# One register load for eight expert width marks on TensorE, in place of eight checked loads

## What is computed

```python
def moe_swiglu(x, router_w, w1, w3, w2):
    logits = (t @ router_w).astype(jnp.float32)
    top_v, top_i = lax.top_k(logits, TOP_K)
    gates = jax.nn.softmax(top_v, axis=-1)
    combine = jnp.sum(jax.nn.one_hot(top_i, N_EXPERTS) * gates[..., None], axis=1)
    for e in range(N_EXPERTS):
        out = out + combine[:, e:e + 1] * swiglu(t, w1[e], w3[e], w2[e])
```

## Time and profile before

| | us |
|---|---|
| median of 3 executions | 2331.02 |
| lowest, highest | 2330.19, 2338.54 |
| the profiled execution, own time | 2329.96 |
| the profiled execution, span from first to last instruction | 2328.0 |
| TensorE busy in the span | 2162.3 (93%) |
| VectorE, ScalarE, GpSimd busy | 1401.6, 1116.9, 1186.8 |

### The profile page before, as it was taken

The page is one execution under the profiler, slowest core; times in us unless marked ns, Lnnn a source line. Parts: engine busy times, 40 slices in busy tenths (PEclk is TensorE's granted clock), DMA queues, the critical chain, the costliest instruction groups (busy, mean ns, idle before and its releaser), DMA issues.

```text
span 2328.0 us, 26804 instructions
## 1 busy us (share of the span) xinstructions
PE 2162.3 (93%) x10612; PEld 1733.7 (74%) x10612; DVE 1401.6 (60%) x1775; ACT 1116.9 (48%) x1117; POOL 1186.8 (51%) x473
## 2 busy tenths in 40 slices
PE   8999899989997899999999999999899996878997
PEld 7578588875775677777778777888678773747997
DVE  4565643355656577777777775433477775455665
ACT  1232334312321576767676674434376772535544
POOL 0120154301200698989899895554398991203443
PEclk9999999989997899999999999999999997979999
DMA  8200464522004598989999896555399893215560
GB/s 303 72 1 18 166 222 156 199 96 73 1 27 166 214 362 326 366 310 360 331 344 360 318 361 223 181 181 183 144 356 358 319 357 122 105 36 187 194 215 21
DMA packets 208094, 484.93 MB, mean 208 GB/s; under 512 B 9168, under 2 KB 13008, under 8 KB 206928
## 3 DMA queue, kind: packets, MB, share of 16 engines
q1 hardware_dynamic: 207952, 483.02, 57.2%
HBM read 481.96 MB, written 1.05 MB: 207 GB/s over the span
## 4 chain that ended last, share of the span: by engine, by line
PE 85%; DVE 8%; ACT 2%; issue 2%; POOL 1%; DMA 1%; DVEq 0%; ACTq 0%; SPq 0%; POOLq 0%
PE bank L949 21%; PE bank L951 20%; PE bank L950 20%; PE bank L586 11%; PE bank L778 5%; PE bank L593 3%; DVE b_arena L1325 1%; PE bank L739 1%; DVE b_X L1325 1%; POOL b_arena L2632 1%; ACT e_hi L2168 1%; DVE b_arena L1331 1%; PE bank L856 1%; PE bank L695 1%; PE bank L1218 1%
## 5 line engine op out<-in xcount | busy, mean ns | idle before, releaser
L2725 POOL TENSOR_TENSOR e_lo<-b_ring,e_hi 128x512 fp32r<-128x512 f32 (+1 forms) x401 | 1122.2, 2819 | 634.6 <-ACT e_hi L2168 634.6
L1797 DVE TENSOR_TENSOR e_lo<-b_ring,e_hi 128x1536 fp32r<-128x1536 f32 (+2 forms) x407 | 781.6, 1921 | 472.2 <-ACT e_hi L2168 468.7
L2168 ACT ACTIVATE e_hi<-b_ring 128x2048 fp32r<-128x2048 f32 (+1 forms) x407 | 777.1, 1912 | 333.0 <-PE bank L951 327.0
L949 PE MATMUL bank<-e_hi,e_xh 128*128 128x512 f32 (+1 forms) x1200 | 475.9, 397 | 31.0 <-POOL e_lo L2725 9.4
L951 PE MATMUL bank<-e_hi,e_xl 128*128 128x512 f32 (+1 forms) x1200 | 466.3, 389 | 0.0
L950 PE MATMUL bank<-e_lo,e_xh 128*128 128x512 f32 (+1 forms) x1200 | 465.8, 388 | 0.0
L949 PEld LDWEIGHTS bank<-e_hi,e_xh 128*128 128x128 f32 x1200 | 226.3, 189 | 97.5 <-issue 50.1
L949 PE MATMUL bank<-e_hi,e_th 128*128 128x512 f32 x688 | 272.1, 396 | 0.7
L950 PE MATMUL bank<-e_lo,e_th 128*128 128x512 f32 x688 | 268.6, 390 | 0.0
L951 PE MATMUL bank<-e_hi,e_tl 128*128 128x512 f32 x688 | 268.6, 390 | 0.0
L951 PEld LDWEIGHTS bank<-e_hi,e_xl 128*128 128x128 f32 x1200 | 226.4, 189 | 48.3
(11 more groups left out here) (233 smaller groups left out, 2351.3 us busy)
## 6 DMA issues: line engine op xcount, KB each, us to landing
b_ring<-in_moe_w SPq DMA_DIRECT2D x168, 2048.0 KB, 8.0
b_ring<-in_w_in SPq DMA_DIRECT2D x15, 2048.0 KB, 9.0
b_ring<-in_ffn_w SPq DMA_DIRECT2D x15, 2048.0 KB, 7.9
b_ring<-in_w_up SPq DMA_DIRECT2D x12, 2048.0 KB, 7.9
b_ring<-in_w_down SPq DMA_DIRECT2D x6, 2048.0 KB, 8.9
b_ring<-in_w_o SPq DMA_DIRECT2D x4, 2048.0 KB, 7.7
b_gain<-in_gains SPq DMA_DIRECT2D x7, 1024.0 KB, 4.7
b_ring<-in_w_out SPq DMA_DIRECT2D x2, 2048.0 KB, 8.3
```

The source lines that it names most:

```text
L949: e.matmul(out, ah, bh, start=first, stop=False)
L1797: e.tensor_tensor(lo[:, 0:at], raw[:, 0:at], r32(hi[:, 0:at]), ALU.subtract).then_inc(lo_dve.sem)
L2168: return e.activation(out, x, ACT.Copy)
L2725: e.tensor_tensor(lo[:, at:], raw[:, at:], r32(hi[:, at:]), ALU.subtract).then_inc(lo_pool.sem)
```

## The change

Now one load instruction fills eight registers from the eight words, and the checks are left out, with the reason that a comparison can only give 0 or 1.

```diff
-                wide = [e.to_reg(e.value_load(flag[0:1, ex:ex + 1], min_val=0, max_val=1)) for ex in range(NE)]
+                wide = [e.to_reg(v) for v in nc.values_load_multi_w_load_instructions(flag[0:1, 0:NE], [e.engine], min_val=0, max_val=1,
+                                                                                           skip_runtime_bounds_check_because="a comparison gives 0 or 1")[1]]
```

## The result

| | before | after |
|---|---|---|
| median of 22 executions each, us | 2331.74 | 2328.04 |
| lowest, highest | 2328.56, 2338.54 | 2323.89, 2333.37 |
| span of the profiled execution | 2328.0 | 2326.7 |

The ratio is 0.998 with a 95% interval of 0.9974 to 0.9987, that is 3.0 to 6.1 us less. The forecast was 4.0 us less, at 2327.0, in a range of 2324.0 to 2331.5. The direction is clear of the noise, and the size is under the 0.5% that the forecast called no change.

A forecast was written before the change was run, and what follows sets the result against it. TensorE's sequencer (marks, hint, branch) was taken to hold expert 0's first product. Saving 764.3 - 760.35 = 3.95, rounded to 4.0 us, with nothing for clock or handing back, gave 2331.0 - 4.0 = 2327.0 us, range 2324.0 to 2331.5.

The forecast's parts named there:

- The place: Ahead of expert 0's first product, 762.03 to 768.55 us: only TensorE's own sequencer holds it back, for 6.5 us.
- Rival 2: Expert 0's first product does wait for GpSimd's `e_lo` at 766.82; 1.6 us gained, 2329.4; chance 0.05.
- What goes: At the marks, 24 sequencer instructions become one load, put at 1.45 us; saves 4.0 us (3.0 to 4.9).
- What stays: Hint and first branch stay; the branch keeps 3.53 us and expert 0's first product follows 0.62 later, at 764.5.
- The clock: TensorE's low-clock stretch at expert 0's start again lasts 4.55 us under work; term nothing, ends 1.9 us lost, 2.1 gained.
- Handed back: After expert 0's first product, no later wait takes the gain back; all 4.0 us stay.
- the prediction's last sign: Expert 1's branch comes near 889.3 us in place of 893.3.
- Rival 3: TensorE's code shifts by 23 instructions; six later hinted branches may miss fetches, 2.8 us each, 2343.9 for all; chance 0.05.
- The time: Whole kernel: median 2327.0 us after the change, from 2331.0 before.

The follow-up runs named there:

- single-part kernels: Kernel before with one eight-word load but checks kept, or eight loads without checks: first product 12.87 and 11.87 us behind the gathers' start; execution times not compared.

## Why the prediction was right, by its steps

**The place.** Right. The chain of waits named GpSimd's `e_lo` ahead of the product; the buffers said that it was not needed. In the changed kernel the product starts at 760.47, with GpSimd on the piece in question from 760.00 until 762.85. Rival 2 is refuted by that row alone. The profiles of both single-part kernels name it again: the product of the eight unchecked loads has a bracket with GpSimd, though its branch ended at 755.8 + 3.84 = 759.6 and the product followed 0.6 later, at 760.25, as in every kernel where the branch is last. Its timeline:

```profile
760.25 0.77 PE L949 MATMUL bank<-e_hi,e_xh 128*128 128x512 f32 x1 [5.60 <-POOL e_lo L2726]
```

**What goes.** The load was put at 1.45 us between ends of 0.50 and 2.4, and is 0.78. That term was 0.67 us too large, as the middle was taken where the runs lie near the end of "further words cost almost nothing": (0.78 - 0.50) / 7 = 0.04 us per further word. By the Trainium skill's figure ("Runtime: NRT & Kernel Launch", "Instruction fetch mechanics", about 200 ns for each register) it would have been 1.6 us; these runs show half (0.78), and the measurement decides.

**What stays.** The branch was put at its one known value, 3.53 us, and was 3.90. This term was 0.37 too small and offset half of the first error, with 0.2 more in small gaps. Predicted from the load's start to the product: 1.45 + 0.1 + 3.53 + 0.62 = 5.7; measured 760.47 - 754.9 = 5.6. That 4.0 predicted and 4.1 measured are so close is in part luck: with the branch of the second profile of before (5.04) the same difference would be 5.8 us. The prediction took one value of a fetch for the value. It should have carried it with bounds, as it did the load.

**The clock.** The term was taken as nothing between -1.9 and 2.1. Windows of the changed kernel, the idle end, the low stretch, and the high one:

```profile
757.30:760.40 3.10, 0.00 (x0) 0.00 (x0) 1.53 (x4) 1.94 (x2) 0.40 (x1) 0.76 0.02 5
760.40:765.70 5.30, 5.24 (x12) 4.18 (x13) 1.31 (x1) 0.00 (x0) 2.45 (x1) 0.50 0.01 3
765.70:769.00 3.30, 3.30 (x16) 2.69 (x15) 1.05 (x1) 2.19 (x2) 1.01 (x1) 1.00 0.00 0
```

The low level (0.50, 1.2 GHz) lasted 5.24 us under work, where it lasted 4.55, a loss of 0.7 x 0.47 = 0.3 us. The prediction's reason, that the clock rises behind the start of work and not at a point of the program, is borne out: in the eight profiles with a late hint it rose 2.9 to 5.8 us behind the first product, whether that came 8.7 or 24.9 us behind the gathers. But one value was taken for the length here too. In the second profile of the kernel before the low stretch ended 2.9 us behind the product of 770.48, and by the next gap 0.75 of the 1.69 us that this product was late had been made up. Its idle end, low and high stretch:

```profile
764.80:770.40 5.60, 0.00 (x0) 0.00 (x0) 1.15 (x1) 0.00 (x0) 2.27 (x1) 0.50 0.05 6
770.40:773.40 3.00, 2.92 (x7) 2.37 (x8) 0.00 (x0) 0.00 (x0) 0.00 (x0) 0.50 0.03 5
773.40:777.00 3.60, 3.60 (x17) 2.94 (x17) 0.11 (x1) 1.93 (x1) 0.06 (x1) 1.00 0.00 0
```

So the 0.3 us are less than what the clock varies by in one program.

**Handed back.** Up to the next gap nothing was, as expected. ScalarE's fourth split waits 6.07 us for TensorE in place of 9.86 and comes 5.5 us behind the first product, where it came 5.2 behind. The next gap's product is 3.8 us earlier (28.70 to 24.94), which is 4.1 less the clock's 0.3. Expert 1's branch, the prediction's last sign, is 3.7 us earlier against 4.0 forecast, from 138.8 (893.3 - 754.49) to 135.1 us (885.6 - 750.51) behind the gathers. The marks read three times show the same in the other direction and to the end of the program.

Behind expert 1's branch there is a loss that the prediction did not look for. Expert 1 takes 129.8 us in both profiles of the kernel before and 131.3 in both of the changed one. TensorE waits 2.34 us there for a signal of VectorE (line 1962, 1963 with the change) in all of them; behind this wait its clock is still high before, and low for 3.3 us with the change. Before, then after:

```profile
899.88 0.47 PE L949 MATMUL bank<-e_hi,e_xh 128*128 128x512 f32 x1 [2.34 <-DVEq L1962]
```

```profile
892.13 0.77 PE L949 MATMUL bank<-e_hi,e_xh 128*128 128x512 f32 x1 [2.34 <-DVEq L1963]
```

It does not go with the instructions that the change removes. Of the other six profiles the two parts alone, load and hint early, and the eight checked loads early lose it too; the marks read three times, and the load early with the hint late, don't. The other half of the fourth stretch's 3.1 us lies in expert 5 (261.2 us before, 262.7 with the change), and that one is spread of one program: the second profile of the kernel before has 262.5. Whether the changed kernel loses the 1.5 us of expert 1 each time is not shown. If it did, 4.1 - 0.3 - 1.5 = 2.3 us would be left, which lies under the 3.0 to 6.1 of the medians.

**Rival 3.** Expert 1's branch and the six later ones, first to last: 0.36, 0.36, 0.33, 0.33, 0.08, 3.54 and 0.35 us in the changed kernel, against 0.36, 0.36, 0.33, 0.33, 0.08, 3.18 and 0.35 before. A shift of 23 instructions harmed none of the six short ones. The long one, which was long before as well, took 3.54 and 3.56 us in the two profiles of the changed kernel and 3.18 and 3.32 in those of the kernel before; over all ten profiles it spreads from 3.08 to 3.63. It isn't an empty worry, though. With the marks read three times the code moves 48 instructions the other way, and there the branch of expert 1 took 1.72 us behind its hint:

```profile
L1145 PEldq COMPARE_BRANCH  x1: 1720/1720/1720, 898.8 to 898.8; - x1
```

That is one value, half the price that was put on such a miss. Whether the shift caused it was not tried apart.

**The time.** 2328.04 against 2327.0. The median before moved too, from 2331.02 (3 executions) to 2331.74 (22), so that 3.7 us (3.0 to 6.1 by the ratio) stand against the 4.0 forecast.

## What to carry to other kernels

When a product starts late, list what it reads and when each was ready before believing the name in the bracket; if all are old, look at the engine's own sequencer: here a register load cost 0.3 us, a check 0.3 us, and a branch with a late hint 3.5 to 5.0 us. Fill registers with one load, leave out checks on values that cannot be out of range, and above all put loads and branch hints where the engine waits anyway: the move gave 2.7 us more at the product than the change did, and with all eight loads and checks kept it already gave 3.5 of the change's 4.1 us. Where single executions spread by several us, judge a change of 4 us in its own stretch, from a point just ahead of it, and enlarge it (here threefold marks) to show that it reaches the end.

## What the runs showed of the hardware

- A load of eight words into registers took 0.78 us (0.79 at most in five profiles), one of a single word 0.30 (0.50 for the first of a row). The two instructions of a bounds check took 0.31 us of the sequencer.
- The first branch, with its hint right ahead of it, took 3.5 to 5.0 us, and 5.04 and 3.53 in the same program. With its hint 5.6 us ahead it took 0.69, with its hint 4.3 us ahead 1.51 (one profile each).
- Where the gap closed the clock gave time back, a term that the expectation of that run left out. In the kernel with load and hint early the granted clock is 1.00 from the product on, behind a pause of 0.85 us, and the first product took 0.50 us in place of 0.77:

```profile
755.00:761.00 6.00, 5.93 (x26) 4.92 (x27) 3.03 (x5) 3.92 (x3) 3.68 (x2) 1.00 0.01 3
```

From the first product to that behind the next gap it took 12.5 us (755.07 to 767.61), where it took 14.6 before and 15.0 with the change. Of the 8.9 us that this kernel had gained by then, 6.8 came from the earlier product and 2.1 from the clock. The kernel with the eight checked loads early shows the same: a pause of 0.85 us, a first product of 0.50, and 12.6 us to the next gap's product (761.00 to 773.56). That the clock's part reached the end is not shown: by the ratio 6.3 us did (4.2 to 8.6), less than the 8.9 of this profile, which is of the fastest execution.
